# The first two weight chunks multiplied tile by tile beside the first modulation vectors, and the shift vector made as a row

## The chip, the cores and the metric

The kernel runs on one core of one Trainium2 chip. The metric is the device time of a run in microseconds. The core has five engines with a queue each, which work side by side and meet only at semaphores: TensorE (PE in the rows; its weight loads are PEld), VectorE (DVE), ScalarE (ACT), GpSimd (POOL) and SyncE (SP), which here only starts the transfers from HBM. All of SP's transfers share 16 DMA engines.

## The reference

Two transformer blocks of two layers each are computed one after the other for a sequence of 512 tokens of width 1024. The change concerns the very beginning of the first block: the vectors `mod` are made from the condition `c`, `x` is modulated with them, and the result goes into a SwiGLU.

```python
def _modulate(x, shift, scale):
    return x * (1.0 + scale) + shift

def _swiglu(h, w_gate, w_up, w_down):
    return (jax.nn.silu(h @ w_gate) * (h @ w_up)) @ w_down
...
    cond = jax.nn.silu(c)
    for l in range(DEPTH):
        mod = cond @ w_ada[l] + b_ada[l]
        sh1, sc1, g1, sh2, sc2, g2, sh3, sc3, g3 = jnp.split(mod[:, None, :].astype(x.dtype), N_MOD, axis=-1)
        y = _swiglu(_modulate(x, sh1, sc1), ffn1_w_gate[l], ffn1_w_up[l], ffn1_w_down[l])
        x = _post_norm(x, y, g1, FFN_RES, ln_gain[l, 0], ln_bias[l, 0])
...
```

Behind this stand the token mixer and the second SwiGLU of each layer, and then the whole second block.

## The kernel before

Everything is fp32, and activations lie transposed in SBUF: `XR`, `HH` and the like hold 8 row tiles of 128 features by 512 tokens. A product with the precision of fp32 is made of three fp32r matmuls: both operands are split into a high part (rounded to fp32r) and a low part (the difference), and `mul3` adds high x high, high x low and low x high. `HH` and `HL` are the two parts of the modulated input `h`, `WH` and `WL` those of a weight chunk, `AH` and `AL` those of the activation.

Weights come in chunks of 1 MB (128 x 2048: 8 row tiles k by 256 output features). A chunk lands in one of `NS` = 3 places of `STAGE`. ACT copies it into `WH` (step `split`, L1719), VectorE subtracts into `WL` (`low`, L2030); there are `NW` = 2 places for the parts. A chunk of 256 output features is 2 output tiles x 8 k x 3 = 48 matmuls of 512 columns. Chunk 0 is the first 256 features of the gate projection, chunk 1 the same of the up projection, chunk 2 the next of the gate, chunk 3 of the up, chunk 4 is one of `w_ada` (for later modulation vectors, which VectorE makes from `STAGE` itself), chunk 5 is of the gate again.

The order of the work is written out in advance by the class `Plan`, a list of named steps with arguments. Each engine then walks over the whole list and emits its own function for a step, if it has one, so the list sets the order in every queue. `Plan.take` hands out a chunk, and before that adds the `split` and `low` of the chunks up to one ahead. `banks` and `tmp` are rings of PSUM banks and of six temporary 128 x 512 tiles.

The opening is three steps. `ada_first` makes the first 16 of the modulation columns: `w_ada` comes in 8 chunks of 256 outputs; chunks 0 to 3 give the shift, 4 to 7 the scale. Four of them (0, 1, 4, 5) are made by TensorE (`ada_pe`: the weights are stationary, the condition is a moving column of one), four (2, 3, 6, 7) by VectorE (`ada_rows`, L2043 to L2049: products by the condition's column, added over k) and summed over the partitions by TensorE with a moving vector of ones (`ada_sum`). `ada_bias` (L2054) adds the bias. `modulate_first` (step `mod_first`) makes `1 + scale` for all eight tiles (L2060) and then `HH` (VectorE, L2065), a copy in full precision (ACT, L1735) and `HL` as their difference (VectorE L2023 for odd tiles, POOL L2581 for even ones), and ACT scales `XR` by ALPHA (L1739). Then the SwiGLU takes chunk 0: an eager `feat2` runs k by k over both output tiles (step `mm2`). Behind a chunk of the gate ACT makes the SiLU from PSUM (step `act`, L1743), behind one of the up VectorE multiplies (`glu`, L2206), and `a_part` splits the product (ACT L1719 for `AH`, POOL L2618 for `AL`). All matmuls of projections are issued in one line, L1385.

Of the kernel before, what the change touches and what calls it, by code (L numbers as in the profile page):

```python
# [105 lines left out]
class Plan:  # L106
# [375 lines left out]
    def ffn(self, kind, names, l, groups, gate, mean, norm=None, nxt=None, root=None, raw=None):  # L482
# [4 lines left out]
        for gi, (g0, G) in enumerate(groups):  # L487
            self.av += 1
            av, a = self.av, gi % 2
            for mi in range(G // 2):  # L490
                idx, first = l * names["n_up"] + g0 // 2 + mi, gi == 0 and mi == 0
                qs = []
                if first and norm:
# [7 lines left out]
                    self.small.free(su, ("glu", pid2), ("act", pid))  # L501
                    continue
# [863 lines left out]
def xe(n, v):  # L1366

    return ("x", n, v) if v else ("x.load",)


def mod_events(l, which):

    if l == 0 and which == 0:
        return [("mod", 0, 0), ("mod", 0, 1), ("mod", 0, 2)]
    if l == 0 and which == 1:
        return [("mod", 0, 4), ("mod", 0, 5), ("mod", 0, 6)]
    return [("mod", l, 4 * which), ("mod", l, 4 * which + 2)]
# [3 lines left out]
def tensor(e, m, plan):  # L1381
# [310 lines left out]
    def hn_out(l, X, heads, i, y, b, sg):  # L1692
# [5 lines left out]
        mm=mm, mm2=mm2, mmt=mmt, ada_pe=ada_pe, ada_sum=ada_sum, ln_mean=ln_mean, ln_var=ln_var,  # L1698
# [16 lines left out]
def scalar(e, m, plan):  # L1715
# [14 lines left out]
    def mod_first(s, hv, qs):  # L1730
        sh, _ = m.MOD[:, 0:8], None
        e.wait_ge(("mod1",))
        for n in range(NT):
            e.wait_ge(("x.load",), qs[n].after)
            act.activation(m.tmp(qs[n]), m.XR[:, n, :], ACT.Identity, bias=sh[:, n:n + 1],  # L1735
                           scale=m.small(s)[:, n:n + 1]).then_inc(*e.up("act_h", "h.q", hv, n))
        for n in range(NT):
# [235 lines left out]
    def x_vcopy(l, c, pid, b):  # L1973
# [5 lines left out]
        begin=begin, split=split, mod_first=mod_first, act=act_, a_part=a_part, xsq=xsq, xg=xg, ln_sub=ln_sub,  # L1979
# [9 lines left out]
def vector(e, m, plan):  # L1989
# [67 lines left out]
    def mod_first(s, hv, qs):  # L2057
        sc, sh, one = m.MOD[:, 8:16], m.MOD[:, 0:8], m.small(s)
        e.wait_ge(mod_events(0, 1), mod_events(0, 0), s.after)
        dve.tensor_scalar(one[:, 0:8], sc, 1.0, None, ALU.add).then_inc(*e.up("dve_mod", "mod1"))  # L2060
        e.wait_ge(("mod1",))
# [1063 lines left out]
```

## Time and profile before

| | |
|---|---|
| median of 3 runs | 3650.49 us |
| lowest and highest of them | 3641.54 and 3650.66 us |
| time of the profiled execution | 3651.82 us |
| its span | 3650.5 us |
| TensorE busy | 3562.9 us, 98% |
| VectorE busy | 1899.3 us, 52% |
| ACT busy | 1234.1 us, 34% |
| POOL busy | 500.3 us, 14% |
| moved by DMA | 373.45 MB, a mean of 102 GB/s |

The span goes from the first to the last instruction that the profiler saw; the time of the execution has 1.3 us more around it. A busy share is a mean over the whole kernel, and says nothing of a single stretch; the opening is read from the timeline.

### The profile page before, as it was taken

Reading aid. Unit: us, or ns where it says so; the run is one execution under the profiler, and the core shown is the slowest. Engines: PE = TensorE matmul, PEld = TensorE weight load, DVE = VectorE, ACT = ScalarE, POOL = GpSimd, SP = SyncE. Lnnn points to the kernel's source line nnn. Section 1 sums busy time; section 2 is a strip of 40 time slices with the busy share of each in tenths; the row PEclk is TensorE's granted clock in tenths of the full one; section 3 lists DMA queues with packets and bytes.
Section 4 is the critical chain, followed back from the end, with each engine's and each line's share of the span. In section 5 each row is a group of like instructions: output and inputs, shape, how many; then the busy total and the mean of one; then the engine's idle time right before and its main releaser. Section 6 shows DMA issues by size and latency. Waiting matters only on the chain.

```text
span 3650.5 us, 41572 instructions
## 1 busy us (share of the span) xinstructions
PE 3562.9 (98%) x16972; PEld 2894.5 (79%) x16972; DVE 1899.3 (52%) x3303; ACT 1234.1 (34%) x1654; POOL 500.3 (14%) x437
## 2 busy tenths in 40 slices
PE   8999999999999999999999999978999999999999
PEld 7888877788888888867788888645888888888887
DVE  4555742664556445644653255686553344564433
ACT  2222472442225222552442234334442223342221
POOL 1010220110012000221210011111111111201111
PEclk9999999999999999999999999978999999999999
DMA  6444311134443344210132212100212222222221
GB/s 253 173 173 173 105 58 57 47 123 154 162 144 111 141 161 160 81 58 35 68 138 93 101 67 81 58 1 34 95 59 103 93 102 89 103 80 93 93 104 69
DMA packets 52608, 373.45 MB, mean 102 GB/s; under 512 B 5825, under 2 KB 5953, under 8 KB 9538
## 3 DMA queue, kind: packets, MB, share of 16 engines
q1 hardware_dynamic: 52418, 370.79, 28.3%
q8 instruction: 134, 2.20, 0.2%
q14 instruction: 56, 0.46, 0.0%
HBM read 368.67 MB, written 2.10 MB: 102 GB/s over the span
## 4 chain that ended last, share of the span: by engine, by line
PE 45%; DVE 4%; ACT 1%; issue 1%; POOL 0%; DVEq 0%; ACTq 0%; POOLq 0%
PE ps L1385 44%; PE ps L1405 0%; DVE s_bm L2426 0%; DVE s_sm L2424 0%; ACT s_tmp L1865 0%; DVE s_tmp L2285 0%; DVE s_tmp L2275 0%; ACT s_wh L1719 0%; DVE s_hl L2023 0%; DVE s_sm L2283 0%; DVE s_xr L2155 0%; DVE s_tmp L2444 0%; DVE s_xx L2285 0%; DVE s_sm L2263 0%; DVE s_tmp L2457 0%
## 5 line engine op out<-in xcount | busy, mean ns | idle before, releaser
L1385 PE MATMUL ps<-s_hh,s_wh 128*128 128x512 f32 x2552 | 1014.9, 398 | 15.2 <-POOL s_hl L2581 10.3
L1385 PE MATMUL ps<-s_hl,s_wh 128*128 128x512 f32 x2552 | 999.6, 392 | 0.0
L1385 PE MATMUL ps<-s_hh,s_wl 128*128 128x512 f32 x2552 | 999.6, 392 | 0.0
L2030 DVE TENSOR_TENSOR s_wl<-s_stage,s_wh 128x2048 fp32r<-128x2048 f32 (+1 forms) x276 | 623.7, 2260 | 654.4 <-ACT s_wh L1719 654.3
L1719 ACT ACTIVATE s_wh<-s_stage 128x2048 fp32r<-128x2048 f32 (+1 forms) x276 | 519.5, 1882 | 617.1 <-PE ps L1385 432.0
L1385 PEld LDWEIGHTS ps<-s_hh,s_wh 128*128 128x128 f32 x2552 | 482.8, 189 | 138.0 <-issue 36.6
L1385 PEld LDWEIGHTS ps<-s_hh,s_wl 128*128 128x128 f32 x2552 | 482.6, 189 | 103.1
L1385 PEld LDWEIGHTS ps<-s_hl,s_wh 128*128 128x128 f32 x2552 | 483.1, 189 | 98.9 <-issue 1.7
L1385 PE MATMUL ps<-s_ah,s_wh 128*128 128x512 f32 x1408 | 561.5, 399 | 0.0
L1385 PE MATMUL ps<-s_ah,s_wl 128*128 128x512 f32 x1408 | 549.6, 390 | 0.0
L1385 PE MATMUL ps<-s_al,s_wh 128*128 128x512 f32 x1408 | 549.0, 390 | 0.0
L2618 POOL TENSOR_TENSOR s_al<-s_tmp,s_ah 128x512 fp32r<-128x512 f32 x152 | 197.7, 1304 | 1691.3 <-ACT s_ah L1719 1691.3
L1385 PEld LDWEIGHTS ps<-s_ah,s_wl 128*128 128x128 f32 x1408 | 264.0, 188 | 57.7
L1385 PEld LDWEIGHTS ps<-s_al,s_wh 128*128 128x128 f32 x1408 | 264.5, 188 | 53.6 <-issue 1.9
L1385 PEld LDWEIGHTS ps<-s_ah,s_wh 128*128 128x128 f32 x1408 | 264.4, 188 | 53.4 <-issue 1.4
L1719 ACT ACTIVATE s_ah<-s_tmp 128x512 fp32r<-128x512 f32 x152 | 96.2, 634 | 572.2 <-DVE s_tmp L2206 312.9
L2083 DVE TENSOR_TENSOR s_xr<-ps,s_xr 128x512 f32<-128x512 f32 x96 | 66.2, 690 | 197.0 <-PE ps L1385 196.9
L2046 DVE SCALAR_TENSOR_TENSOR s_tmp<-s_stage,s_cond,s_tmp 128x256 f32<-128x256 f32 x384 | 157.4, 480 | 0.0
L2081 DVE SCALAR_TENSOR_TENSOR s_xr<-ps,s_sm,s_xr 128x512 f32<-128x512 f32 x112 | 83.3, 748 | 120.4 <-PE ps L1385 119.9
L1743 ACT ACTIVATE s_tmp<-ps 128x512 f32<-128x512 f32 x82 | 49.1, 598 | 259.4 <-PE ps L1385 259.3
L2206 DVE TENSOR_TENSOR s_tmp<-s_tmp,ps 128x512 f32<-128x512 f32 x82 | 55.7, 685 | 117.7 <-PE ps L1385 117.7
L1385 PEld LDWEIGHTS ps<-s_cc,s_tmp 128*128 128x128 f32 x760 | 102.0, 206 | 11.5 <-ACT s_tmp L1854 3.0
(432 smaller groups left out, 3783.1 us busy)
## 6 DMA issues: line engine op xcount, KB each, us to landing
s_stage<-in_w_ada SPq DMA_DIRECT2D x64, 1024.0 KB, 4.8
s_stage<-in_ffn_w_gate SPq DMA_DIRECT2D x44, 1024.0 KB, 4.8
s_stage<-in_ffn_w_up SPq DMA_DIRECT2D x44, 1024.0 KB, 4.8
s_stage<-in_ffn_down SPq DMA_DIRECT2D x32, 1024.0 KB, 4.8
s_stage<-in_w_up SPq DMA_DIRECT2D x32, 1024.0 KB, 4.8
s_stage<-in_down_m SPq DMA_DIRECT2D x32, 1024.0 KB, 4.7
s_stage<-in_w_in SPq DMA_DIRECT2D x24, 1024.0 KB, 4.8
s_stage<-in_ffn_down SPq DMA_DIRECT2D x16, 768.0 KB, 4.2
```

The lines of the kernel that those rows point to most:

```text
L1385: return pe.matmul(out, lhs, rhs, start=start, stop=stop, skip_group_check=True)
L1719: return act.activation(out, src, ACT.Copy)
L1743: act.activation(m.tmp(q), m.bank(b), ACT.Silu).then_inc(*e.up("act_ffn", "act", pid))
L2030: ins = dve.tensor_tensor(m.WL[:, ws, a:z], m.STAGE[:, j % NS, a:z], m.WH[:, ws, a:z].bitcast(F32), ALU.subtract)
L2046: ins = dve.scalar_tensor_tensor(dst, w[:, k, :], cond, dst, ALU.mult, ALU.add)
L2081: ins = dve.scalar_tensor_tensor(x, m.bank(b), m.small(gate[0])[:, n:n + 1], x, ALU.mult, ALU.add)
L2083: ins = dve.tensor_tensor(x, m.bank(b), x, ALU.add)
L2206: dve.tensor_tensor(m.tmp(q), m.tmp(q), m.bank(b), ALU.mult).then_inc(*e.up("dve_ffn", "glu", pid))
L2618: pool.tensor_tensor(m.AL[a][:, k, :], m.tmp(q), m.AH[a][:, k, :].bitcast(F32), ALU.subtract).then_inc(*e.up("pool_a", "a.lo", av, k))
```

## The change

`ada_first` and `modulate_first` are gone, and so is the ordinary handling of the first two chunks in `ffn`. In their place `opening` runs four times over a pair p of row tiles (2p and 2p + 1):

- VectorE makes the sums for the scale's chunk p + 4 (`ada_rows`), as it did for half of the chunks before.
- TensorE makes the shift's chunk p as a row (`ada_row`): the condition's column k is stationary (128 x 1), 256 columns of `WA` are moving, 8 matmuls add up into one partition of a bank. ACT copies the row into SBUF, and `ada_turn` turns it into two columns (stationary: 128 elements of the row, moving: one element of `one`). `ada_col` sums the scale's two columns over the partitions.
- VectorE adds both biases and makes `1 + scale` for the two tiles (`mod_pair`), and `mod_h` modulates the two tiles.
- The parts of chunk 0 and chunk 1 (one k, both output tiles, 6 matmuls) are placed around this, those of chunk 1 one pair later, in the place where TensorE's queue stands before a wait.

The transfers follow that order: `x` comes in four quarters, the two first weight chunks behind the first pair, the constants `cc` behind all of it; `one` is no constant from HBM any more but set by POOL. Both activation tiles of chunks 0 and 1 come behind the opening.

```diff
+    def opening(self, gate, up):
+        self.add("begin")
+        for p in range(4):
+            self.add("wa_load", p + 4)
+            self.add("wa_load", p)
+            self.add("x_load", p)
+            if p == 0:
+                self.issue(0)
+                self.issue(1)
+        self.issue(2)
+        self.add("begin_c1")
+        self.order += [(*gate, False, False), (*up, False, False)]
+        self.taken = self.nsplit = 2
...
+        def part(i, k):
+            ch, pid, kt, n, bs, x, ver, ks, wide = runs[i]
+            self.add("mm2", pid, ch, kt, n, bs, x, ver, ks, wide, k, k + 1)
+
+        for p in range(4):
+            b, row, acc, q = self.banks.take(), self.tmp.take(), self.tmp.take(), self.tmp.take()
+            self.add("ada_rows", 0, p + 4, None, acc, q)
+            self.tmp.free(q, ("ada", 0, p + 4))
+            if p < 2 and self.stream:
+                part_of = self.split(p)
+            self.add("ada_row", p, b, row)
+            if p < 2 and self.stream:
+                self.add("low", *part_of)
+            if p:
+                part(1, 2 * p - 2)
+            self.add("ada_turn", p, b, row)
+            self.add("ada_col", p + 4, acc, b)
+            self.add("mod_pair", p, b, s)
+            qs = [self.tmp.take(), self.tmp.take()]
+            self.add("mod_h", p, s, self.hv, qs)
...
+            if p:
+                part(1, 2 * p - 1)
+            part(0, 2 * p)
+            part(0, 2 * p + 1)
+        self.release(chunks[0], ("proj", runs[0][1] + 1))
+        part(1, 6)
+        part(1, 7)
...
+                if first and kind == "swiglu":
+                    one, two = self.opening((names["gate"], idx), (names["up"], idx))
+                    for (b, pid), (b2, pid2), col in zip(one, two, range(2)):
+                        q = self.tmp.take()
+                        self.add("act", pid, b, q)
+                        self.banks.free(b, ("act", pid))
+                        self.add("glu", pid2, pid, b2, q)
+                        self.banks.free(b2, ("glu", pid2))
+                        self.add("a_part", av, a, col, q, ("glu", pid2), afree[a])
...
+    def ada_row(c, b, q):
+        e.wait_ge(("wa", c), ("cond",), b.after)
+        for k in range(8):
+            ins = mul(m.bank(b)[0:1, 0:256], m.COND[:, k:k + 1], m.WA[:, c, k * 256:k * 256 + 256], k == 0, k == 7)
+        ins.then_inc(*e.up("pe_ada", "ada.row", c))
+
+    def ada_turn(c, b, q):
+        e.wait_ge(("row", c), ("one",))
+        for j in range(2):
+            ins = mul(m.bank(b)[:, 256 + j:257 + j], m.tmp(q)[0:1, j * P:(j + 1) * P], m.one[0:1, :])
+        ins.then_inc(*e.up("pe_ada", "ada.sum", 0, c))
+
+    def ada_col(c, acc, b):
+        e.wait_ge(("ada", 0, c))
+        for j in range(2):
+            at = c % 2 * 256 + j * P
+            ins = mul(m.bank(b)[:, 258 + j:259 + j], m.tmp(acc)[:, at:at + P], m.one)
+        ins.then_inc(*e.up("pe_ada", "ada.sum", 0, c))
...
+    def mod_pair(p, b, s):
+        e.wait_ge(("ada.sum", 0, p), ("ada.sum", 0, p + 4))
+        for c, at in ((p, 256), (p + 4, 258)):
+            dve.tensor_tensor(m.MOD[:, 2 * c:2 * c + 2], m.bank(b)[:, at:at + 2], m.vec("b_ada", 2 * c, 2), ALU.add).then_inc(
+                *e.up("dve_mod", "mod", 0, c))
+        e.wait_ge(("mod", 0, p + 4), s.after)
+        dve.tensor_scalar(m.small(s)[:, 2 * p:2 * p + 2], m.MOD[:, 8 + 2 * p:10 + 2 * p], 1.0, None, ALU.add).then_inc(
+            *e.up("dve_mod", "mod1", p))
```

TensorE's queue at its start. Before, 64 one-column matmuls of `w_ada` and 8 of the sums stand ahead of the first matmul of `h` (`s_hh` and `s_hl` are its parts, `s_wh` and `s_wl` those of the chunk; the names behind "waits" are semaphores):

```order
L1385 MATMUL ps<-s_cond,s_wa 128x1 [waits barrier_Pool_Activation_PE_DVE_SP_release,q_act_misc,q_wa0]
L1385 MATMUL ps<-s_cond,s_wa 128x1 x15
L1385 MATMUL ps<-s_cond,s_wa 128x1 [waits q_wa1]
L1385 MATMUL ps<-s_cond,s_wa 128x1 x15
L1385 MATMUL ps<-s_cond,s_wa 128x1 [waits q_wa4]
L1385 MATMUL ps<-s_cond,s_wa 128x1 x15
L1385 MATMUL ps<-s_cond,s_wa 128x1 [waits q_wa5]
L1385 MATMUL ps<-s_cond,s_wa 128x1 x15
L1385 MATMUL ps<-s_cc,s_tmp 128x1 [waits q_cc,q_dve_ada]
L1385 MATMUL ps<-s_cc,s_tmp 128x1 x3
L1385 MATMUL ps<-s_cc,s_tmp 128x1 [waits q_dve_ada]
L1385 MATMUL ps<-s_cc,s_tmp 128x1 x3
L1385 MATMUL ps<-s_hh,s_wh 128x512 [waits q_dve_mod,q_pool_h,q_dve_w]
```

Of the change, from the second pair's row of shifts on (`s_wa,s_cond`), with the columns (`s_one,s_tmp`) behind one part of chunk 1:

```order
L1415 MATMUL ps<-s_wa,s_cond 1x256 [waits q_wa1]
L1415 MATMUL ps<-s_wa,s_cond 1x256 x7
L1415 MATMUL ps<-s_hh,s_wh 128x512 [waits q_dve_w]
L1415 MATMUL ps<-s_hl,s_wh 128x512
L1415 MATMUL ps<-s_hh,s_wl 128x512
L1415 MATMUL ps<-s_hh,s_wh 128x512
L1415 MATMUL ps<-s_hl,s_wh 128x512
L1415 MATMUL ps<-s_hh,s_wl 128x512
L1415 MATMUL ps<-s_one,s_tmp 128x1 [waits q_act_misc]
L1415 MATMUL ps<-s_one,s_tmp 128x1
L1415 MATMUL ps<-s_one,s_tmp 128x1 [waits q_dve_ada]
L1415 MATMUL ps<-s_one,s_tmp 128x1
```

What moved: the modulation work no longer stands ahead of all matmuls of `h`, but in four portions between them, and each portion's columns are followed by one more part of chunk 1 before the next wait for `HL`.

ACT's queue around the first two chunks before (L1719 on `s_wh` is the split of chunk 1, then of chunk 2; L1743 is the SiLU, L1719 on `s_ah` the high part of the activation; L1739 scales `XR`):

```order
L1739 ACTIVATE s_xr<-s_xr 128x512 [waits q_act_h,q_dve_hh] x8
L1719 ACTIVATE s_wh<-s_stage 128x2048 [waits q_st1]
L1743 ACTIVATE s_tmp<-ps 128x512 [waits q_pool_h,q_pe_proj]
L1743 ACTIVATE s_tmp<-ps 128x512 [waits q_dve_h,q_pe_proj]
L1719 ACTIVATE s_wh<-s_stage 128x2048 [waits q_st2]
L1719 ACTIVATE s_ah_68<-s_tmp 128x512 [waits q_dve_ffn] x2
L1719 ACTIVATE s_wh<-s_stage 128x2048 [waits q_pe_proj,q_st0]
```

ACT's queue of the change, from the last pair's row copy (L1760 on a 1x256 form) on; L1788 is the SiLU and L1760 the copy to `s_ah` and `s_wh`:

```order
L1760 ACTIVATE s_tmp<-ps 1x256 [waits q_dve_h,q_pe_ada]
L1780 ACTIVATE s_tmp<-s_xr,s_mod,s_sm 128x512 [waits q_dve_ada,q_x3,q_dve_mod]
L1780 ACTIVATE s_tmp<-s_xr,s_mod,s_sm 128x512 [waits q_pool_h]
L1784 ACTIVATE s_xr<-s_xr 128x512 [waits q_act_h,q_dve_hh] x2
L1788 ACTIVATE s_tmp<-ps 128x512 [waits q_dve_h,q_pe_proj]
L1760 ACTIVATE s_ah_69<-s_tmp 128x512 [waits q_dve_ffn]
L1788 ACTIVATE s_tmp<-ps 128x512 [waits q_pe_ada,q_pe_proj]
L1760 ACTIVATE s_ah_69<-s_tmp 128x512 [waits q_dve_ffn]
L1760 ACTIVATE s_wh<-s_stage 128x2048 [waits q_st2]
L1760 ACTIVATE s_wh<-s_stage 128x2048 [waits q_pe_proj,q_st0]
```

What moved: the split of chunk 2 stood ahead of the activation's high parts and does now stand behind both of them.

## Rows read from the trace of the kernel before

**Rows 1.** The page, part 1: busy us (share of the span) xinstructions
```profile
PE 3562.9 (98%) x16972; PEld 2894.5 (79%) x16972; DVE 1899.3 (52%) x3303; ACT 1234.1 (34%) x1654; POOL 500.3 (14%) x437
```

**Rows 2.** Windows, opening and first two chunks: busy (count) by engine, TensorE clock, DMA share, GB/s
```profile
0.00:41.80 41.80, 30.88 (x144) 30.79 (x144) 18.89 (x47) 5.67 (x7) 1.47 (x5) 1.00 0.97 400
41.80:65.40 23.60, 23.56 (x96) 19.40 (x97) 13.16 (x13) 13.25 (x18) 6.11 (x4) 1.00 0.37 136
```

**Rows 3.** Timeline of the opening: start us, us, engine, line, instruction, count [idle before, releaser]
```profile
6.14 27.46 PE L1385 MATMUL ps<-s_cond,s_wa 128*128 128x1 f32 x128 [6.14 <-DMA s_wa<-in_w_ada]
...
8.60 0.61 DVE L2043 TENSOR_SCALAR s_tmp<-s_wa,s_cond 128x256 f32<-128x256 f32 x2 [8.60 <-DMA s_wa<-in_w_ada]
...
11.62 0.42 DVE L2049 TENSOR_TENSOR s_tmp<-s_tmp 128x256 f32<-128x256 f32 x1
...
24.95 0.62 DVE L2043 TENSOR_SCALAR s_tmp<-s_wa,s_cond 128x256 f32<-128x256 f32 x2 [1.53 <-DMA s_wa<-in_w_ada]
...
33.69 1.91 ACT L1719 ACTIVATE s_wh<-s_stage 128x2048 fp32r<-128x2048 f32 x1 [30.35 <-DMA s_stage<-in_ffn_w_gate]
...
37.05 0.16 DVE L2054 TENSOR_TENSOR s_mod<-ps,s_vec 128x4 f32<-128x4 f32 x1 [1.54 <-PE ps L1385]
37.13 2.28 DVE L2030 TENSOR_TENSOR s_wl<-s_stage,s_wh 128x2048 fp32r<-128x2048 f32 x1
39.33 0.17 DVE L2060 TENSOR_SCALAR s_sm<-s_mod 128x8 f32<-128x8 f32 x1
...
39.53 2.44 DVE L2065 TENSOR_SCALAR s_hh<-s_xr,s_sm,s_mod 128x512 fp32r<-128x512 f32 x3
40.43 1.27 POOL L2581 TENSOR_TENSOR s_hl<-s_tmp,s_hh 128x512 fp32r<-128x512 f32 x1 [39.99 <-ACT s_tmp L1735]
...
41.84 0.77 PE L1385 MATMUL ps<-s_hh,s_wh 128*128 128x512 f32 x1 [4.82 <-POOL s_hl L2581]
```

**Rows 4.** Timeline, single matmuls of the first chunk
```profile
42.83 0.63 PE L1385 MATMUL ps<-s_hh,s_wl 128*128 128x512 f32 x1
...
43.26 0.63 PE L1385 MATMUL ps<-s_hh,s_wh 128*128 128x512 f32 x1
...
45.76 0.39 PE L1385 MATMUL ps<-s_hh,s_wh 128*128 128x512 f32 x1
...
45.98 0.39 PE L1385 MATMUL ps<-s_hl,s_wh 128*128 128x512 f32 x1
```

**Rows 5.** Timelines of VectorE and ACT, 50 to 75 us
```profile
57.26 2.29 DVE L2030 TENSOR_TENSOR s_wl<-s_stage,s_wh 128x2048 fp32r<-128x2048 f32 x1 [3.46 <-ACT s_wh L1719]
60.26 0.69 DVE L2206 TENSOR_TENSOR s_tmp<-s_tmp,ps 128x512 f32<-128x512 f32 x1 [0.71 <-PE ps L1385]
...
68.90 2.29 DVE L2030 TENSOR_TENSOR s_wl<-s_stage,s_wh 128x2048 fp32r<-128x2048 f32 x1 [2.51 <-ACT s_wh L1719]
...
60.98 0.64 ACT L1719 ACTIVATE s_ah<-s_tmp 128x512 fp32r<-128x512 f32 x1 [3.76 <-DVE s_tmp L2206]
66.42 0.64 ACT L1719 ACTIVATE s_ah<-s_tmp 128x512 fp32r<-128x512 f32 x1 [4.81 <-DVE s_tmp L2206]
66.96 1.90 ACT L1719 ACTIVATE s_wh<-s_stage 128x2048 fp32r<-128x2048 f32 x1
71.14 0.60 ACT L1743 ACTIVATE s_tmp<-ps 128x512 f32<-128x512 f32 x1 [2.27 <-PE ps L1385]
```

**Rows 6.** Timelines of TensorE near 109 and 484 us: small fp32 matmuls
```profile
109.02 0.95 PE L1385 MATMUL ps<-s_cc,s_tmp 128*128 128x1 f32 x8
...
484.48 1.57 PE L1385 MATMUL ps<-s_nk,s_cc 128*128 128x256 f32 x8
485.81 0.47 PE L1385 MATMUL ps<-s_hh,s_wh 128*128 128x512 f32 x1
```

**Rows 7.** Windows of TensorE alone in an attention stage of the second block
```profile
2450.00:2460.00 10.00, 5.87 (x29) 0.67 0.00 0
2640.00:2650.00 10.00, 8.17 (x49) 1.00 0.01 2
```

More of the change, by code:

```diff
@@ L1366, in xe @@
 def xe(n, v):
-    return ("x", n, v) if v else ("x.load",)
+    return ("x", n, v) if v else ("x.load", n // 2)
 def mod_events(l, which):
[L1373 to L1376, printed above, removed]
     return [("mod", l, 4 * which), ("mod", l, 4 * which + 2)]
@@ L1728, in split, with ada_row, mod_h @@
         copy(m.WH[:, ws, 0:n], m.STAGE[:, j % NS, 0:n]).then_inc(*e.up("act_w", "w.hi", j))
[L1730 to L1735, printed above, removed]
+    def ada_row(c, b, q):
+        e.wait_ge(("ada.row", c), q.after)
+        copy(m.tmp(q)[0:1, 0:256], m.bank(b)[0:1, 0:256]).then_inc(*e.up("act_misc", "row", c))
+    def mod_h(p, s, hv, qs):
+        sh = m.MOD[:, 0:8]
+        e.wait_ge(("mod1", p), ("x.load", p))
+        for n in (2 * p, 2 * p + 1):
+            e.wait_ge(qs[n % 2].after)
+            act.activation(m.tmp(qs[n % 2]), m.XR[:, n, :], ACT.Identity, bias=sh[:, n:n + 1],
                            scale=m.small(s)[:, n:n + 1]).then_inc(*e.up("act_h", "h.q", hv, n))
-        for n in range(NT):
+        for n in (2 * p, 2 * p + 1):
             e.wait_ge(("h.hi", hv, n), ("h.q", hv, n))
@@ L2055, in ada_bias, with mod_h @@
             *e.up("dve_mod", "mod", l, c))
[L2057 to L2061, printed above, removed]
[L2062 to L2069 removed]
+    def mod_pair(p, b, s):
[6 more added lines that the diff above has]
+            *e.up("dve_mod", "mod1", p))
+    def mod_h(p, s, hv, qs):
+        sh, one = m.MOD[:, 0:8], m.small(s)
+        e.wait_ge(("mod1", p), ("x.load", p))
+        for n in (2 * p, 2 * p + 1):
+            dve.tensor_scalar(m.HH[:, n, :], m.XR[:, n, :], one[:, n:n + 1], sh[:, n:n + 1], ALU.mult, ALU.add).then_inc(
+                *e.up("dve_hh", "h.hi", hv, n))
+        e.wait_ge(("h.q", hv, n))
+        h_low(hv, n, m.tmp(qs[1]))
     def gate(l, which, w, s):
@@ L2582, in h_low, with begin, mod_h @@
             *e.up("pool_h", "h.lo", hv, n))
-    def mod_first(s, hv, qs):
-        for n in range(0, NT, 2):
-            e.wait_ge(("h.q", hv, n))
-            h_low(hv, n, m.tmp(qs[n]))
+    def begin():
+        pool.memset(m.one, 1.0).then_inc(*e.up("pool_one", "one"))
+    def mod_h(p, s, hv, qs):
+        e.wait_ge(("h.q", hv, 2 * p))
+        h_low(hv, 2 * p, m.tmp(qs[0]))
     def xsum(sid, n, v, v0, acc):
@@ L2970, in consts @@
     cc["ident"] = np.eye(P, dtype=f)
-    cc["one"] = np.ones((P, 1), f)
     cc["later"] = (i[:, None] > i[None, :]).astype(f)
```

86 lines of the change are left out of this document (29 added, 57 removed).

## The prediction

> **What bounds the kernel now.** I read the page first, then the stretches, then the timeline of the opening. The page shows TensorE busy for 3562.9 us, 98% of the span [rows 1]: the time is that of a stream of matmuls, and only what moves the start of that stream, or opens a hole in it, counts. The largest single place where the stream is missing is the opening. In its first 41.8 us the DMA engines are busy 0.97 of the time, while TensorE's 30.88 us are one-column products that only make modulation vectors [rows 2]. The timeline shows the chain [rows 3]: the first `w_ada` chunk lands at 6.14, the second at 8.60 (2.46 us for each), the last of eight at 24.95; the first gate chunk comes after `x`, at 33.69; its high part takes 1.91, its low part 2.28 from 37.13; `1 + scale` follows at 39.33, the modulated row tiles from 39.53, and the first real matmul at 41.84, when POOL has made the low part of row tile 0.
>
> From there the first nine matmuls start 0.43 us apart and the later ones 0.227 apart [rows 4], which is 512 columns at 1.2 GHz and then at 2.4 GHz (the granted clock column says 1.00 in both [rows 2]; the steps decide). Chunks 0 and 1 have 96 matmuls. Nine take 3.92 us, 87 take 19.7, so **chunk 2 starts at 65.5**. Nothing waits between: the split of a chunk is always done one chunk ahead.
>
> **The change, part by part.** *Transfers.* The order is now `w_ada` 4, 0, a quarter of `x`, gate, up, and then two `w_ada` chunks and a quarter of `x` for each further pair. At 2.46 us per chunk and half of that per quarter, `w_ada` 0 lands at 8.6, the gate chunk at about 12.3, up at 14.8, `w_ada` 3 at about 32 and the last quarter at about 34. The rows after 24.95 ran later than this pace, so up to 1.5 us more is possible.
>
> *First pair.* ACT makes the gate's high part from 12.3 to 14.2, then copies the row out of PSUM (no such copy is in the rows; between VectorE's 0.16 us for four columns and ACT's 0.60 for 128x512 [rows 3, 5]; 0.4 taken, which the wait for the low part covers). VectorE's low part is done at 16.6. TensorE makes the row of shifts from 8.7, is done by 14 even at the low clock (below), and turns it into two columns and sums the scale's two columns: eight records of the one-column kind, 27.46/128 = 0.215 us each at the low clock [rows 3], to 16.6. Then bias and `1 + scale` (0.16 + 0.17 and the step to 39.53: 0.5 [rows 3]), and 2.31 us from the start of the modulation to the first matmul, as 39.53 to 41.84 [rows 3]. The first real matmul starts at **19.6**, 22 us earlier than before.
>
> *What a pair costs after that.* On TensorE's one queue each further pair is: the row of shifts R; one part of chunk 1 (six matmuls, 1.36); the columns, eight records in 0.95 us at the high clock [rows 6], 0.9 taken; then the wait for bias, `1 + scale` and modulation, 0.1 + 0.5 + 2.31 = 2.9, of which one part of chunk 1 hides 1.36; then two parts of chunk 0, 2.72. For R there is no row: one stationary column and 256 moving fp32 columns. The nearest are fp32 matmuls of 256 columns with a full stationary tile, eight records between 484.48 and 485.81, 0.166 us each [rows 6]; two records for each instruction make 16 for a row, 2.66. Below, 256 columns at 2.4 GHz take 0.107, so 1.7. Above, twice the first, 5.3, at the low clock. I take 2.5, near the row. A pair is then 2.5 + 1.36 + 0.9 + 2.9 + 2.72 = 10.4 us, so it is TensorE's order and one latency that set the pace, not the transfers: pair 3 is reached at about 45, its data lie there by 34. VectorE's sum for the next scale (8.60 to 12.04, 3.4 us [rows 3]) starts as soon as the low part of a pair's second tile is made, and fits beside 2.72 + 2.5 + 1.36; in the second pair the low part of `up` (2.3) is behind it, and the 5.7 still fit into 6.6. The low clock over the first nine matmuls costs 9 x 0.2 = 1.8 again.
>
> The Trainium skill says (TensorE: Matmul & The Clock Gate, LDWEIGHTS) that the load of a stationary operand takes time by its columns, whatever its rows; a one-column load would be nearly free, R would be 1.7 and the sum below 2.4 us lower. No row before shows such a load.
>
> Both chunks end at T = 19.6 + 1.8 + 2.72 + 3 x 10.4 + 2.72 = **58.0**, against 65.5.
>
> *The hole behind them.* The opening takes both chunks itself, and the split of chunk 2 stands behind both activation tiles in ACT's queue. Before, it ran while chunk 1 was multiplied, its low part from 57.26 [rows 5], eight us early. Now, from T, by the steps of [rows 5]: VectorE's product of tile 0 at T - 0.5, the high part of the activation 0.72 later, the next activation 0.54 after that, the next product 0.6, the next high part 0.72, the split 0.54, the low part 1.94 later and 2.29 long. TensorE can start chunk 2 at T + 7.0 = 65.0. A pause of 4.8 us before 41.84 was followed by nine steps at the low clock [rows 3, 4]; after 7 us I charge the same 1.8 once more. That is **66.8** against 65.5: a loss of 1.3 us. Later splits keep their order, the low part of chunk 5, the next gate chunk, is ready some 6 us early, and TensorE, ACT and VectorE have the same order from there, but for which temporary buffer is used. The earlier start carries nothing beyond.
>
> *Other edits.* `one` by a memset on POOL, `cc` after the last stage load, the loss of 64 - 32 and the gain of 16 - 8 small matmuls are inside the terms above. The scaling of `x` by ACT is in the waits of a pair.
>
> The sum against the profiled execution is 3651.8 + 1.3 = 3653.1. The runs' median is 1.3 below it, so I expect a median near **3652**. One of the three runs was 9 us below the others, which this sum can't explain.
>
> **Rivals.** *1. The wash (0.66):* start gained, hole paid, within 5 us: 3647 to 3657. For it: all terms but R have rows.
>
> *2. The clock stays low through the opening, on the other side (0.14 for enough of it to be slower by over 0.3%, 0.10 for less).* Before, 27 us of one-column products on a TensorE that was never idle left it at 1.2 GHz, at 0.215 a record where the high clock gives 0.12 [rows 3, 6]. In the new opening rows and columns are a third of each pair and another 1.6 us are idle. If that holds the clock low throughout, R is at least 4.4 (16 records of 256 columns at 1.2 GHz, 0.213, and the same 0.06 that 0.166 has over 0.107), a part 2.56, the columns 1.7: a pair is 4.4 + 2.56 + 1.7 + 2.9 + 5.1 = 16.7, T = 19.6 + 5.1 + 50 + 5.1 = 80 and the start of chunk 2 lies near 89, so 3651 + 23 = 3675. It decides from about half of the pairs at the low level. Elsewhere the trace speaks both ways: 5.87 us busy of 10 had a granted clock of 0.67, 8.17 of 10 had 1.00 [rows 7]; a pair has 8.8 of 10.4 busy. The Trainium skill's page (the same title, Part 1: The HAM clock gate) has the clock fall after idle time; no pause in a pair is as long as the 4.8 us seen before 41.84.
>
> *3. The hole isn't there (0.04):* were the split ready in time, chunk 2 would start at 58.0, 7.5 us earlier: 3643. Against it: ACT's order. Even this is within 0.3%.
>
> To be faster by more than 0.3% (11 us, about what a measurement of this kernel can tell from no change), chunk 2 would have to start at 54 with no cold start; transfers alone allow it, no order of these queues that I see does. I leave 0.04 for it, as scatter like that of the low run. The last 0.02 are for the other side: transfers that land 1.5 us late at the first pair, the shifted temporary buffers and a high run together.
>
> **The numbers.** Range 3642 to 3663: below, rival 3 and a low run; above, nearly two pairs at the low clock (6.3 us each). The likeliest case alone is 3647 to 3657. Within 0.3% are 0.66 + 0.10 + 0.04 = 0.80, slower 0.14 + 0.02 = 0.16, faster 0.04.
>
> **What the changed profile would show.** First real matmul near 19.6 (wrong by over 2: the first pair's chain). Pairs 10.4 apart, with 256-column records of 0.11 to 0.17 us; 0.27 and steps of 0.43 would be rival 2. No wait for a transfer from the second pair on. ACT's third split after both activation tiles, and TensorE waiting some 7 us for the low part of chunk 2, then nine steps of 0.43. Chunk 2 near 65 to 67. If it starts before 60 or after 75, the prediction is wrong.

## The result, and the profile after it

The changed kernel took 3652.84 us, the median of 20 runs (3646.77 to 3666.09), against 3645.65 for the kernel before, 20 runs on the same chip (3638.23 to 3655.26). The ratio is 1.0018 with a 95% interval of 1.0009 to 1.0026: within 0.3%, and on the slow side of it. In a second comparison on one chip (changed_again, below) it was 1.0006 (0.9995 to 1.0017). The profiled execution took 3656.54 us, its span is 3655.2.

The page, part 1, where TensorE has 4 us less than in [rows 1]:

```profile
PE 3558.9 (97%) x16924; PEld 2874.3 (79%) x16924; DVE 1899.0 (52%) x3308; ACT 1233.9 (34%) x1658; POOL 501.9 (14%) x438
```

The two windows of [rows 2]. The DMA engines are as busy in the first, and TensorE's 18.74 us in the second stretch have 85 matmul records where 96 stood:

```profile
0.00:41.80 41.80, 27.16 (x109) 15.04 (x109) 19.59 (x41) 11.33 (x15) 2.85 (x7) 0.96 0.97 393
41.80:65.40 23.60, 18.74 (x85) 12.61 (x84) 9.82 (x23) 7.44 (x13) 3.81 (x3) 1.00 0.25 105
```

Its timeline of the opening, to be laid beside [rows 3]; a start, a length, and in brackets what the engine waited for:

```profile
13.10 1.91 ACT L1760 ACTIVATE s_wh<-s_stage 128x2048 fp32r<-128x2048 f32 x1 [9.72 <-DMA s_stage<-in_ffn_w_gate]
15.33 1.14 PE L1415 MATMUL ps<-s_one,s_tmp 1*128 1x1 f32 x8 [0.97 <-ACT s_tmp L1760]
...
20.02 0.77 PE L1415 MATMUL ps<-s_hh,s_wh 128*128 128x512 f32 x1 [3.56 <-POOL s_hl L2630]
24.34 3.61 PE L1415 MATMUL ps<-s_wa,s_cond 128*1 128x256 f32 x16
27.88 0.50 PE L1415 MATMUL ps<-s_hh,s_wh 128*128 128x512 f32 x1
29.47 1.14 PE L1415 MATMUL ps<-s_one,s_tmp 1*128 1x1 f32 x8
30.47 0.48 PE L1415 MATMUL ps<-s_hh,s_wh 128*128 128x512 f32 x1
33.40 0.50 PE L1415 MATMUL ps<-s_hh,s_wh 128*128 128x512 f32 x1 [1.32 <-POOL s_hl L2630]
36.35 3.61 PE L1415 MATMUL ps<-s_wa,s_cond 128*1 128x256 f32 x16
...
62.76 0.39 PE L1415 MATMUL ps<-s_hh,s_wl 128*128 128x512 f32 x1
69.97 0.79 PE L1415 MATMUL ps<-s_hh,s_wh 128*128 128x512 f32 x1 [6.83 <-DVE s_wl L2075]
70.56 0.63 PE L1415 MATMUL ps<-s_hl,s_wh 128*128 128x512 f32 x1
...
74.32 0.39 PE L1415 MATMUL ps<-s_hl,s_wh 128*128 128x512 f32 x1
```

Chunks 0 and 1 start 22 us earlier and are done at 63.0, 2.5 us before they were (65.5). Chunk 2 then waits to 69.97. A pair takes 12.0 us (24.34 to 36.35): the row 3.54, one part of chunk 1 1.59, the columns 1.00, the wait 2.93, two parts of chunk 0 2.95. ACT's timeline shows why chunk 2 waits, and what has come of it by its SiLU, which stood at 71.14 in [rows 5]:

```profile
59.78 0.60 ACT L1788 ACTIVATE s_tmp<-ps 128x512 f32<-128x512 f32 x1 [2.03 <-PE ps L1415]
63.23 0.63 ACT L1760 ACTIVATE s_ah<-s_tmp 128x512 fp32r<-128x512 f32 x1 [2.84 <-DVE s_tmp L2255]
63.76 0.58 ACT L1788 ACTIVATE s_tmp<-ps 128x512 f32<-128x512 f32 x1
65.16 0.63 ACT L1760 ACTIVATE s_ah<-s_tmp 128x512 fp32r<-128x512 f32 x1 [0.82 <-DVE s_tmp L2255]
65.70 3.69 ACT L1760 ACTIVATE s_wh<-s_stage 128x2048 fp32r<-128x2048 f32 x2
77.72 0.60 ACT L1788 ACTIVATE s_tmp<-ps 128x512 f32<-128x512 f32 x1 [8.32 <-PE ps L1415]
```

71.14 to 77.72 is 6.6 us later: 4.5 for the later start of chunk 2, and 2.1 for its first ten steps, 4.35 us where ten steps of 0.227 take 2.27. The kernel loses 6.6 us in its first 78, and 7.2 by the medians.

### The profile page after: what moved, and what is told of

Same layout as the page of the kernel before. It is cut to its first block, busy times and chain, and to the rows that moved or that the text cites. A ratio compares the mean times of both kernels' runs of the same rounds, so it can differ in the third digit from the quotient of the medians.

```text
span 3655.2 us, 41497 instructions
## 1 busy us (share of the span) xinstructions
PE 3558.9 (97%) x16924; PEld 2874.3 (79%) x16924; DVE 1899.0 (52%) x3308; ACT 1233.9 (34%) x1658; POOL 501.9 (14%) x438
## 4 chain that ended last, share of the span: by engine, by line
PE 44%; DVE 4%; ACT 1%; issue 1%; POOL 0%; DVEq 0%; ACTq 0%; POOLq 0%
PE ps L1415 44%; PE ps L1435 0%; ACT s_tmp L1910 0%; DVE s_bm L2475 0%; DVE s_sm L2473 0%; DVE s_tmp L2334 0%; DVE s_tmp L2324 0%; DVE s_tmp L2493 0%; ACT s_wh L1760 0%; DVE s_sm L2332 0%; DVE s_hl L2068 0%; DVE s_xr L2204 0%; DVE s_sm L2312 0%; DVE s_sm L2327 0%; DVE s_xx L2334 0%
## 5 line engine op out<-in xcount | busy, mean ns | idle before, releaser
L1415 PE MATMUL ps<-s_hh,s_wh 128*128 128x512 f32 x2552 | 1017.2, 399 | 24.7 <-POOL s_hl L2630 12.9
L1760 ACT ACTIVATE s_wh<-s_stage 128x2048 fp32r<-128x2048 f32 (+1 forms) x276 | 519.0, 1881 | 598.5 <-PE ps L1415 444.5
L1760 ACT ACTIVATE s_ah<-s_tmp 128x512 fp32r<-128x512 f32 x152 | 95.9, 632 | 565.8 <-DVE s_tmp L2255 306.5
L1788 ACT ACTIVATE s_tmp<-ps 128x512 f32<-128x512 f32 x82 | 48.9, 596 | 265.3 <-PE ps L1415 265.3
L2239 DVE TENSOR_TENSOR s_tmp<-ps,s_c 128x512 f32<-128x512 f32 x64 | 44.1, 689 | 118.9 <-PE ps L1415 105.4
```

The source lines that it names most:

```text
L1415: return pe.matmul(out, lhs, rhs, start=start, stop=stop, skip_group_check=True)
L1760: return act.activation(out, src, ACT.Copy)
L1788: act.activation(m.tmp(q), m.bank(b), ACT.Silu).then_inc(*e.up("act_ffn", "act", pid))
L2239: dve.tensor_tensor(x, m.bank(b), m.RB, ALU.mult).then_inc(*e.up("dve_act", "act", pid))
```

## Experiments

My theory after the result: TensorE's order sets the opening; the row of shifts is dearer than I took it, the split of chunk 2 comes too late, and the pause costs a stretch at 1.2 GHz besides. **Shift** below is the start of chunk 2's first matmul against 65.50, with 2.1 us added where steps of 0.43 follow a pause and 0.2 where full speed does (the first step after a wait is 0.34 long). For the changed kernel it is +6.6.

### The late split, the clock, the row, the columns

*early_split*, the split taken ahead of the activations:

```diff
         self.release(chunks[0], ("proj", runs[0][1] + 1))
+        if self.stream:
+            self.add("low", *self.split(2))
+            self.nsplit = 3
         part(1, 6)
```


> The changed kernel with the split of chunk 2 (ACT's high part, VectorE's low part) placed right behind the end of chunk 0 in the opening, ahead of both activation tiles. Theory 1 (the hole behind the opening is the order of ACT's queue, and its pause costs the low clock besides): chunk 0 ends at 60.3, the high part runs from 60.5, the low part ends at 64.7, chunk 2 starts at 64.8 instead of 69.97 and at steps of 0.227, so everything from chunk 2 on comes 7.1 us earlier than in the changed kernel, and 0.7 earlier than in the kernel before: near 3645 where the changed kernel has 3652.8. Theory 2 (a later limit, transfers or VectorE, gives it back): chunk 2 starts earlier but the shift is gone by 150 us. Theory 3 (the clock falls by any pause): 5.2 us only, with slow steps left.

*keep_clock*, unused matmuls in the hole:

```diff
         part(1, 7)
         self.release(chunks[1], ("proj", runs[1][1] + 1))
+        b = self.banks.take()
+        self.add("spin", b)
+        self.banks.free(b, ("spin",))
...
+        for i in range(28):
+            ins = mul(m.bank(b), m.HH[:, 0, 0:P], m.HL[:, 0, :])
```


> The changed kernel with 28 matmuls of 512 columns into an unused bank behind the last part of chunk 1, 6.4 us, so that TensorE is busy in the hole. Theory 1 (the nine slow steps after the hole are the clock that fell in the pause): chunk 2 still starts at 69.97, but its steps are 0.227 from the first on; 1.9 us less in all. Theory 2 (the slow steps belong to the beginning of a chunk, such as reads beside VectorE's writes): the steps stay at 0.43, no gain.

*short_row*, one of the row's eight products (the shift is then made of an eighth of the condition):

```diff
-        for k in range(8):
-            ins = mul(m.bank(b)[0:1, 0:256], m.COND[:, k:k + 1], m.WA[:, c, k * 256:k * 256 + 256], k == 0, k == 7)
+        for k in range(1):
+            ins = mul(m.bank(b)[0:1, 0:256], m.COND[:, k:k + 1], m.WA[:, c, k * 256:k * 256 + 256], k == 0, k == 0)
```


> The changed kernel with only the first of the eight products of each row of shifts (so the shift leaves out 7 of 8 terms). Theory 1 (the row stands on the path of each later pair, one for one): 3.54 us become 0.44; pairs 2 and 3 are 3.1 us shorter, pair 1 by 1.9 because the low part of the up chunk is ready only at 26.0; both chunks end at 54.9 instead of 63.0, chunk 2 starts at 61.9: 8.1 us less. Theory 2 (VectorE's sums or the transfers set the pace of a pair): between 0 and 2 us less, with TensorE waiting for VectorE's sums or for w_ada instead.

*columns*, the shift made as columns again, inside the new opening:

```diff
-        for k in range(8):
-            ins = mul(m.bank(b)[0:1, 0:256], m.COND[:, k:k + 1], m.WA[:, c, k * 256:k * 256 + 256], k == 0, k == 7)
...
         for j in range(2):
...
+            for k in range(8):
+                ins = mul(m.bank(b)[:, 256 + j:257 + j], m.WA[:, c, k * 256 + j * P:k * 256 + j * P + P],
+                          m.COND[:, k:k + 1], k == 0, k == 7)
```

> The changed kernel, but each shift chunk is made as before, as columns (the weights stationary, the condition a moving column; 16 matmuls in 32 records), with no row copy and no turning. Theory 1 (the row form brings nothing of its own): 32 records of 0.107 to 0.12 are 3.4 to 3.8 us where the row takes 3.54, the turning saves 0.5 a pair; a pair takes 11.4 to 11.8 instead of 12.0, and chunk 2 starts 0.6 to 1.8 us earlier, 68.2 to 69.4; the first real matmul stays at 20.0. Theory 2 (the row form keeps the clock high, one-column products don't): some pairs run at steps of 0.43 and 0.215, and chunk 2 starts 3 to 20 us later.

The timeline of TensorE, early_split, where chunk 2 starts, and then keep_clock:

```profile
65.04 0.50 PE L1418 MATMUL ps<-s_hh,s_wh 128*128 128x512 f32 x1 [1.67 <-DVE s_wl L2078]
65.38 0.39 PE L1418 MATMUL ps<-s_hl,s_wh 128*128 128x512 f32 x1
```
```profile
63.22 6.51 PE L1418 MATMUL ps<-s_hl,s_hh 128*128 128x512 f32 x28
70.22 0.50 PE L1418 MATMUL ps<-s_hh,s_wh 128*128 128x512 f32 x1 [0.50 <-DVE s_wl L2084]
70.57 0.40 PE L1418 MATMUL ps<-s_hl,s_wh 128*128 128x512 f32 x1
```

With the early split the wait is 1.67 us instead of 6.83 and the clock stays up: shift -0.3. The median was 3640.2, 5 us under the 3645 expected, ratio 0.9979 (0.9967 to 0.9991). With the hole filled by work the wait for the same low part is there, but the steps after it are at full speed: the low clock follows the pause, and costs 1.9 us. Shift +4.9, median 3648.29, ratio 1.0003 (0.9989 to 1.0018).

Without seven eighths of the row a pair takes 9.0 us and chunk 2 starts 7.6 us earlier, behind the same hole; in short_row's timeline:

```profile
25.60 0.77 PE L1415 MATMUL ps<-s_wa,s_cond 128*1 128x256 f32 x2
...
34.79 0.59 PE L1415 MATMUL ps<-s_wa,s_cond 128*1 128x256 f32 x2
...
62.36 0.80 PE L1415 MATMUL ps<-s_hh,s_wh 128*128 128x512 f32 x1 [6.82 <-DVE s_wl L2075]
```

Three rows that shrink by 3.0 us each make 9.0, less 1.3 because the clock rose later in the first pair (its row starts at 25.60, not at 24.34). So the row is on the path with its whole length. Shift -1.0, median 3641.29, ratio 0.9977 (0.9965 to 0.999).

The columns are no longer than the row at the high clock (3.63 against 3.61), but they do something else, in columns' timeline:

```profile
23.49 0.39 PE L1414 MATMUL ps<-s_hh,s_wl 128*128 128x512 f32 x1
23.72 4.86 PE L1414 MATMUL ps<-s_cond,s_wa 128*128 128x1 f32 x32
28.44 0.77 PE L1414 MATMUL ps<-s_hh,s_wh 128*128 128x512 f32 x1
29.01 0.63 PE L1414 MATMUL ps<-s_hl,s_wh 128*128 128x512 f32 x1
29.44 0.63 PE L1414 MATMUL ps<-s_hh,s_wl 128*128 128x512 f32 x1
```

Full speed when they begin (0.23 a step), 1.2 GHz when they end (0.43 a step), with no pause between: record by record, the step goes from 0.112 to 0.213 at 25.88, 2.2 us into these columns. The columns of the next pair left the clock up, and those of the last were followed by a second fall 1 us behind their end, again without a pause:

```profile
48.78 3.63 PE L1414 MATMUL ps<-s_cond,s_wa 128*128 128x1 f32 x32
...
53.39 0.63 PE L1414 MATMUL ps<-s_hl,s_wh 128*128 128x512 f32 x1
```

Over the rows of pairs 1 to 3 the clock never fell in any trace of the new opening. So the columns go with a clock that falls in two pairs of three, in one profile; what in them makes it fall is not shown. Chunk 2 starts at 70.45, 0.5 us later than in the changed kernel, where theory 1 had it 0.6 to 1.8 earlier and theory 2, right in kind, 3 to 20 later. Shift +7.1, median 3654.88, ratio 1.0012 (0.9996 to 1.0028).

### The row by itself

*row_alone*: in the kernel before, the four chunks of TensorE's share as rows.

```diff
-            b = self.banks.take()
-            self.add("ada_pe", c, b)
+            b, q = self.banks.take(), self.tmp.take()
+            self.add("ada_row", c, b, q)
+            self.add("ada_turn", c, b, q)
+            self.tmp.free(q, ("ada.sum", 0, c))
...
```


> One part of the change alone, in the kernel before: the four chunks of the shift that TensorE makes come as a row with a stationary vector and are turned, instead of as columns; the order of everything else is as in the kernel before. Theory 1 (before, these products lie beside VectorE's rows and nearly all of their time is hidden): the shift's products are shorter on TensorE, its first product of a chunk of weights starts 0 to 2 us earlier than 41.84, chunk 2 starts 0 to 2 us earlier than 65.5, and the median is within 3 us of the kernel before. Rival (the row form is worth something by itself): over 3 us less at chunk 2. Second rival (the clock stays at its low level without the 64 products of columns, or rises earlier with the rows): chunk 2's start moves by more than the first product's does.

The first real matmul starts at 38.92 instead of 41.84, and chunk 2 at 63.09: shift -2.4, median 3644.8, ratio 0.9985 (0.9971 to 0.9999). A row of 16 records 0.427 apart would take 6.8 us; its timeline shows 5.37 for the first and 3.61 for the third. In the first, the step between records goes from 0.427 to 0.216 at 9.8, so the clock rose while a row ran, where 27 us of columns had never raised it [rows 3]. The second starts at the high clock, 0.5 us after a wait of 3.61 us, falls back to 0.427 a record from 16.8 on and is up again at 20.1:

```profile
6.08 5.37 PE L1387 MATMUL ps<-s_wa,s_cond 128*1 128x256 f32 x16 [6.08 <-DMA s_wa<-in_w_ada]
15.06 0.57 PE L1387 MATMUL ps<-s_cc,s_tmp 1*128 1x1 f32 x4 [3.61 <-DMA s_cc<-in_cc]
15.56 5.30 PE L1387 MATMUL ps<-s_wa,s_cond 128*1 128x256 f32 x16
21.85 3.61 PE L1387 MATMUL ps<-s_wa,s_cond 128*1 128x256 f32 x16
38.92 0.77 PE L1387 MATMUL ps<-s_hh,s_wh 128*128 128x512 f32 x1 [5.91 <-POOL s_hl L2591]
```
```profile
32.27 1.91 ACT L1725 ACTIVATE s_wh<-s_stage 128x2048 fp32r<-128x2048 f32 x1 [1.78 <-DMA s_stage<-in_ffn_w_gate]
34.21 2.29 DVE L2040 TENSOR_TENSOR s_wl<-s_stage,s_wh 128x2048 fp32r<-128x2048 f32 x1 [1.00 <-ACT s_wh L1725]
```

Before, VectorE's low part at 37.13 stood behind a bias at 37.05 that waited for the sums [rows 3], 1.5 us after its high part was ready (33.69 + 1.91); here, in the second fence (ACT and VectorE), it starts as soon as the high part is made. The other 1.4 us is a gate chunk that landed earlier. It came at 33.5 to 33.7 in all four profiles with the old opening (before, rings_shift, delay_one, delay_two), so it belongs to this variant, but I can't explain it. Chunk 2 gains 2.4 and not 2.9, as eleven steps are slow where nine were. Theory 1 bore out in kind; its bound of 2 us is exceeded by that transfer, and the median lies 4.4 us under the kernel before where it allowed 3. The row form has a small worth of its own, 1.5 us, that the prediction had not seen.

### Both mended

*row_ahead*: early_split, and the rows of pairs 2 and 3 put into the wait of the pair before them, with parts of chunk 1 moved behind to suit.

```diff
             self.add("mod_h", p, s, self.hv, qs)
...
-            if p:
-                part(1, 2 * p - 1)
+            if p in (1, 2):
+                row(p + 1)
+            if p == 3:
+                part(1, 3)
+                part(1, 4)
```


> The changed kernel with chunk 2 split ahead of the first activation (as early_split) and with the row of shifts of pairs 2 and 3 put into the wait of the pair before it. Sum from measured steps: the wait of 2.93 us of each pair then covers a row of 3.54 us, and the period of a pair is some 9.0 instead of 12.0 us; the first row ends at 27.9, the last product of chunk 0 at 54.6, both chunks at 58.6, and chunk 2 starts at 59.0 and in steps of 0.23 us at once. Theory 1 (the pairs' chain is TensorE's own: row, turn, wait): chunk 2 starts between 58.5 and 60.0, against 69.97 and slow steps: 12.9 us earlier than in the changed kernel in effect, 6.5 us earlier than in the kernel before, and the median lies 4 to 9 us under the kernel before. Rival (the loads of the chunks' parts or the other engines' pairs hold TensorE up once the rows are gone from the chain): waits for ScalarE, VectorE or a transfer of over 1 us a pair appear, and chunk 2 starts after 62.

In row_ahead's timeline of TensorE:

```profile
40.54 3.61 PE L1430 MATMUL ps<-s_wa,s_cond 128*1 128x256 f32 x16
44.09 0.50 PE L1430 MATMUL ps<-s_hh,s_wh 128*128 128x512 f32 x1
...
59.78 0.50 PE L1430 MATMUL ps<-s_hh,s_wh 128*128 128x512 f32 x1 [0.32 <-DVE s_wl L2090]
```

The chunks' matmuls follow the row with no wait, and chunk 2 starts at 59.78, at full speed: shift -5.5, median 3641.93, ratio 0.9973 (0.9958 to 0.9989). This version beats both kernels, by 0.2 to 0.3%; once more (*ahead_again*) 3642.62, 0.9978 (0.9963 to 0.9992). The 0.8 us above the expected 59.0 is the clock of the first pair: twelve steps of 0.43 in this run, seven in the changed kernel's.

### What a shift of the opening is worth at the end

early_split's median lay 8 us under the kernel before, with a level opening, and the changed kernel's own loss read 7.2 us and then less. Six more runs bear on that.

*changed_again*, unaltered:


> The changed kernel once more, unaltered, on the chip of the three kernels below, since two variants of it came out 7 us under what their opening says. Theory 1 (the opening decides, and what it loses is carried to the end less what the later stages' clock gives back): chunk 2's products start at 69.97 as before, 6.4 us later in effect than in the kernel before, and the median lies 2 to 8 us above the kernel before. Theory 2 (the later stages' clock decides more than the opening): the opening is the same to 0.1 us, and the median still lies within 2 us of the kernel before or below it.


*rings_shift*, the kernel before with the same buffers as the changed one from chunk 2 on:

```diff
         self.small.free(s, ("h.lo", self.hv, NT - 1))
+        for _ in range(2):
+            b = self.banks.take()
+            self.banks.free(b, *(b.after or []))
+        self.tmp.n += 6
```


> The kernel before with one thing changed that carries no work: behind the first modulation the numbers of the rings of PSUM banks and temporary buffers are advanced by what the changed kernel advances them (two banks, six buffers), so that from chunk 2 on every operation uses the same bank and buffer as in the changed kernel. It tells whether the variants' surplus of 7 us is owed to other buffers rather than to the opening. Theory 1 (buffers are alike): chunk 2 starts at 65.5 as before, and the median is within 2 us of the kernel before. Rival (which bank or buffer an operation gets changes waits later on): the opening is the same and the median moves by 3 us or more, with a place of the trace at which the shift against the kernel before appears.


*delay_one* and *delay_two*, the kernel before with 28 or 56 of keep_clock's unused matmuls ahead of chunk 2:


> The kernel before with 28 unused products of 128x512 on TensorE between chunk 1 and chunk 2, 0.227 us each, so that chunk 2 starts 6.4 us later at the high clock, as much later as it effectively does in the changed kernel. It asks what a shift of the opening alone is worth at the end. Theory 1 (a shift of the opening is carried to the end, and the later stages add only scatter): chunk 2 starts at 71.9 and the median lies 4 to 9 us above the kernel before. Theory 2 (the later stages' clock takes back part of a shift, as the changed kernel's 6.4 us came out as 3.5 us in one comparison and 7 us in the other): the median lies 0 to 3 us above.

> The same with 56 unused products, 12.7 us. Theory 1: chunk 2 starts at 78.2 and the median lies 10 to 15 us above the kernel before, and 4 to 9 us above the run with 28. Theory 2 (where the later stages fall against the clock's changes depends on when they begin): the two runs don't lie on one line through zero; one of them is off it by 4 us or more.


*early_again* and *ahead_again*, unaltered:


> The variant early_split once more, unaltered: the opening is level with the kernel before (0.3 us earlier), but its median was 8 us under it. Theory 1 (the opening is all, and the 8 us were scatter): the median now lies within 3 us of the kernel before. Theory 2 (the later stages' clock favours this kernel each time): again 5 us or more under the kernel before.

> The variant row_ahead once more, unaltered: its opening is 5.7 us ahead of the kernel before at chunk 2. Theory 1: the median lies 4 to 9 us under the kernel before, and 3 to 9 us under early_again in the same comparison. Theory 2: it lies within 3 us of early_again, as in the first comparisons of the two, whose medians were 1.7 us apart.

All against the kernel before in their own comparison (medians 3645.65 for the changed kernel, 3648.15, 3649.15 and 3649.74 for the others). The last column is taken from the profiles: the start of VectorE's 121st low part, less that in the kernel before, where it is

```profile
1502.07 2.28 DVE L2030 TENSOR_TENSOR s_wl<-s_stage,s_wh 128x2048 fp32r<-128x2048 f32 x1
```

and in the changed kernel, with as many low parts ahead of it,

```profile
1507.53 2.29 DVE L2075 TENSOR_TENSOR s_wl<-s_stage,s_wh 128x2048 fp32r<-128x2048 f32 x1
```

| run | shift, us | median less that of before | ratio, interval | at 1502 us |
|---|---|---|---|---|
| row_ahead, ahead_again | -5.5, -5.7 | -7.2, -7.1 | 0.9973, 0.9978 | -1.7, -4.7 |
| row_alone | -2.4 | -4.4 | 0.9985 | +1.6 |
| short_row | -1.0 | -6.9 | 0.9977 | +2.4 |
| early_split, early_again | -0.3, 0.0 | -8.0, -7.3 | 0.9979, 0.9987 (0.9973 to 1.0001) | +1.9, -0.7 |
| rings_shift | 0.0 | -0.3 | 0.9995 (0.9984 to 1.0007) | +1.6 |
| keep_clock | +4.9 | +0.1 | 1.0003 | +5.7 |
| delay_one | +6.5 | +10.9 | 1.0025 (1.0009 to 1.0041) | +4.1 |
| changed kernel, changed_again | +6.6, +6.9 | +7.2, +3.5 | 1.0018, 1.0006 | +5.5, +5.5 |
| columns | +7.1 | +6.7 | 1.0012 | +11.6 |
| delay_two | +12.9 | +10.9 | 1.0041 (1.0024 to 1.0059) | +11.4 |

The direction is kept, the size is not. Another numbering of the buffers shows no effect (rings_shift, theory 1). changed_again and delay_two fall into theory 1's ranges, and delay_one 2 us above its own; but delay_two was to lie 4 to 9 us above delay_one, and the two medians are equal. The medians mislead there: nine of delay_one's twelve runs lie between 3656 and 3664 and three at 3645 to 3647, and the ratios, 1.0025 and 1.0041, are 6 us apart, as the delays are. early_split, twice, came out 7 us better than its opening by the median (theory 2), and level with row_ahead, whose opening is 5.5 us ahead of it (theory 2 again); by the ratio the second time is 5 us, and its interval reaches 1.0001. With 12 runs for most of them (7 for delay_two) an interval is 8 to 13 us wide, so single deviations of 4 us say little.

The profiles, one of each run, say more of where a shift goes. At 1502 us it is still there: each kernel's distance from the kernel before is its shift, give or take 4.5 us. Behind that it is not. Between the low parts that stand at 2358 and 2775 us in the kernel before, all the other 13 profiles gain between 5 and 13 us on that of the kernel before: early_split goes from +1.9 to -10.8, changed_again from +5.5 to -4.9, rings_shift from +7.0 to +0.1. So the opening's shift is handed on to the middle of the kernel, and what parts early_split from a level opening arises in the second block.

The place of the scatter can be seen. Two profiles of the same kernel, row_ahead and ahead_again, have spans of 3644.0 and 3630.7 and the same opening. TensorE's windows of two stages of the second block, of the first and then of the second of them (PE busy, records, granted clock, DMA share, GB/s):

```profile
1669.00:1765.00 96.00, 89.83 (x488) 0.84 0.10 38
2320.00:2545.00 225.00, 189.85 (x899) 0.85 0.07 24
```
```profile
1669.00:1765.00 96.00, 89.32 (x527) 0.93 0.12 45
2320.00:2545.00 225.00, 191.59 (x887) 0.82 0.07 25
```

By the issues of the stage transfers, 3.1 us of the 13.3 are there by 755 us, and 7.0 more arise between 1452 and 1828, where the granted clock of the first window is 0.84 in one and 0.93 in the other; the second window hardly differs between these two. Over all 14 profiles the first window had 0.93 in eight, 0.84 or 0.85 in five, 0.89 in one. Such stages with pauses come out now one way and now another, in steps of up to 7 us, and the 100 runs of the kernel before in these comparisons spread by a standard deviation of 6.4 us. That steps lie there is shown; why some kernels meet the better side more often stays open. Eight of the nine comparisons of a kernel with the new opening have a median below its shift, by 0.4 to 7.7 us, so the new opening may also gain something later that the shift doesn't hold. Nothing here tells that from scatter: I tried no kernel that moves only the later stages.

## Why the prediction was right, and where it was not

- **Time and range.** 3652.84 for 3652, inside 3642 to 3663, and a loss within 0.3%, as forecast. That the number fits to 1 us is luck: the forecast stood on 3650.49 for the kernel before, which was 3645.65 in the comparison, and the loss was 6.6 us at chunk 2's SiLU (7.2 by the medians) where the sum had 1.3. The likeliest case had said within 5.
- **First matmul.** 20.02 for 19.6. The gate chunk came at 13.1, not 12.3; the rest of the first pair's chain had 0.4 us to spare.
- **The term that was mis-sized: R, "I take 2.5, near the row".** It measured 3.54, +1.04 three times over, with records 0.216 us apart where 0.11 to 0.17 were given as the sign. The fault was in reading [rows 6]: the row of "128x256 x8" joins two shapes. Grouped by shape, the kernel before shows in that stretch (instructions by shape, busy, mean ns):

```profile
L1385 PE MATMUL ps<-s_nk,s_cc 128*128 128x256 f32 x4 | 1.3, 406 | 0.0
L1385 PE MATMUL ps<-s_nk,s_cc 128*128 128x128 f32 x4 | 0.8, 274 | 0.0
```

  So 1.33 us was for 4 x 256 + 4 x 128 columns, not for 8 x 256. A row of one shape stood 25 us on in the same trace, two records of 512 columns each, 0.43 us apart:

```profile
509.40 1.02 PE L1385 MATMUL ps<-s_rq,s_cc 128*128 128x512 f32 x2
510.26 1.02 PE L1385 MATMUL ps<-s_rk,s_cc 128*128 128x512 f32 x2
```

  (510.26 - 509.40)/2 = 0.43, thus 0.215 for 256 columns and 3.44 for 16 records: within 3% of what came. A pair would have been 11.3, and the loss 4.1. Both bounds, 1.7 and 5.3, had held it.
- **The rest of the pair.** Each part that follows another kind of matmul takes 0.23 more (27.88 to 28.22 is 0.34 where a step is 0.227, and a tenth before it): 1.59 for 1.36, 2.95 for 2.72. This was not in the sum: 0.46 a pair. The wait was 2.93 for 2.9, the columns 1.00 for 0.9.
- **T.** 63.0 for 58.0: 3 x 1.6 from the pairs.
- **The hole.** 63.0 to 69.97, 6.98 for 7.0. This was the sum of eight steps of other engines' queues, taken from [rows 5] (as listed they make 6.85), and the surest part; early_split shows that it was the late split, as argued.
- **The clock after it.** Ten slow steps and 2.1 us for 1.8; keep_clock shows that the pause is the cause. The Trainium skill (TensorE: Matmul & The Clock Gate, Part 1: The HAM clock gate) has the clock fall after idle time, and the trace agrees here.
- **Rival 2** fell: the clock was up from the eighth matmul on, and the pauses of 1.3 us in each pair left it up. But the clock can be lost there: with the old form inside the new opening (columns) it fell twice. The prediction had not kept rows and columns apart.
- **Rival 3.** Even with the early split the low part of chunk 2 is ready only at 65.0, and 1.67 us of wait stay. row_ahead, with 0.32, is the order of the queues that I had said I didn't see.
- **The rule on LDWEIGHTS.** The loads of one column are short, 0.13 at the low clock where a full load there takes 0.33 (below, the changed kernel's timeline), so the rule that the prediction took from the Trainium skill (TensorE: Matmul & The Clock Gate, LDWEIGHTS) holds in its direction. But R is set by the moving columns (records of 256 are 0.216 us apart, records of 512 0.43), and the 1.7 worked out by it was half of what came.

```profile
12.17 0.13 PEld L1415 LDWEIGHTS ps<-s_wa,s_cond 128*1 128x1 f32 x1 [0.30 <-issue]
...
20.59 0.33 PEld L1415 LDWEIGHTS ps<-s_hh,s_wl 128*128 128x128 f32 x1
```

## What to carry to other kernels

Before a row prices a missing operation, split it by shape: a mean over two shapes is the price of neither, and here it cost 3 of the 5.3 us that the sum missed. When a stage is pulled forward, follow the queues past its end: work that was prepared one chunk ahead must still be ordered ahead, or what was gained at the start is paid back in one hole, with a low clock behind it. And when the pauses of later stages make the time of one execution scatter by 6 us, a change of 5 us is judged by the landmark right behind it, in the profile, and only its sign by the median.

## What the runs showed of the hardware

- A true fp32 matmul comes as two records, each at two cycles for a column: 0.43 us for 512 columns at 2.4 GHz, 0.216 for 256, and 3.54 us for 8 matmuls of 256, or about four cycles for a column and matmul. fp32r takes about one (0.227 us for 512). The Trainium skill (FP8 and Floating Point Precision, TensorE Precision Notes) gives true fp32 four passes; the trace agrees, and by it alone R would have been an estimate of 3.4.
- A TensorE without a pause can still lose its clock: it stood at 1.2 GHz over 27 us of matmuls with one moving column [rows 3] and fell from 2.4 during a set of 32 such records (columns, 25.88), though a second set left it up. It rose from 1.2 GHz during the first row of matmuls with one stationary and 256 moving columns (row_alone, 9.8), and in the second of these rows it fell once more, behind a wait of 3.61 us.
- The clock column of a window says 1.00 in stretches whose steps are at 1.2 GHz [rows 2]; in the changed kernel's opening it said 0.96. The steps between equal matmuls are what can be read.
